# Second mixer: an order of their own for VectorE and ScalarE

## What is computed

```python
def sliding_window_sink_attention(q, k, v, sinks):      # 2 blocks of 128 queries, 16 heads on 4 kv heads
    ...
        sc = jnp.einsum('bqhgd,bkhd->bhgqk', qi, ki) * scale
        sc = jnp.where(valid, sc, -jnp.inf)
        mx = jnp.maximum(jnp.max(sc, axis=-1), sink)
        p = jnp.exp(sc - mx[..., None])
        denom = jnp.sum(p, axis=-1) + jnp.exp(sink - mx)
        return jnp.einsum('bhgqk,bkhd->bqhgd', (p / denom[..., None]), vi)

def swa_memory_mixer(...):
    q, q_mem = jnp.split(rms_norm(h, norm_w) @ in_w, [Q_WIDTH], axis=-1)
    q = partial_rope(q.reshape(bsz, s, Q_HEADS, HEAD_DIM), positions)       # rotates 16 of each head's 64
    att = sliding_window_sink_attention(q, k_sh, v_sh, sinks)
    m = memory_cross_attention(q_mem, mem, mem_norm_w, mem_w_kv)            # 4 heads over 256 memory tokens
    return jnp.concatenate([att, m], axis=-1) @ out_w
```

## Time and profile before

| | before |
|---|---|
| median of 3 runs | 1348.51 us (1348.46 to 1349.13) |
| the profiled execution | 1347.25 us |
| its span | 1345.4 us |
| mean granted TensorE clock | 0.964 |
| TensorE busy | 1217.9 us, 91% of the span |
| VectorE, ScalarE, GpSimd busy | 278.3, 210.3, 32.6 us |
| DMA | 463.03 MB, mean 344 GB/s |

### The profile page before, as it was taken

The page is one execution under the profiler, slowest core; times in us unless marked ns, Lnnn a source line. Parts: engine busy times, 40 slices in busy tenths (PEclk is TensorE's granted clock), DMA queues, the critical chain, the costliest instruction groups (busy, mean ns, idle before and its releaser), DMA issues. The chain is left out here.

```text
span 1345.4 us, 15098 instructions
## 1 busy us (share of the span) xinstructions
PE 1217.9 (91%) x6036; PEld 606.6 (45%) x6036; DVE 278.3 (21%) x679; ACT 210.3 (16%) x498; POOL 32.6 (2%) x42
## 2 busy tenths in 40 slices
PE   6999999999999999967777999999999999966785
PEld 5874775544444443532323475554444444322221
DVE  3841552131111111010101235241111111100101
ACT  2223332110000000000003235330010000000002
POOL 0001210000000000000000011100000000000000
PEclk9999999999999999989797999999999999978797
DMA  9830169579999999999999371389999999999994
GB/s 360 329 125 25 48 239 423 189 307 426 427 426 425 428 427 423 426 424 427 427 426 355 146 294 51 118 355 423 421 425 427 426 427 425 426 427 427 426 426 186
DMA packets 81241, 463.03 MB, mean 344 GB/s; under 512 B 7392, under 2 KB 9488, under 8 KB 32016
## 3 DMA queue, kind: packets, MB, share of 16 engines
q1 hardware_dynamic: 81168, 462.02, 83.1%
HBM read 460.91 MB, written 1.07 MB: 343 GB/s over the span
## 5 line engine op out<-in xcount | busy, mean ns | idle before, releaser
L1515 PE MATMUL bank<-own,work 128*64 128x512 f32 (+1 forms) x1176 | 281.0, 616 | 27.3 <-DMA own<-in_w_up 10.5
L1515 PEld LDWEIGHTS bank<-own,work 128*64 128x64 f32 (+1 forms) x1176 | 80.9, 128 | 166.6 <-issue 166.6
L1515 PE MATMUL bank<-late,work 128*32 128x512 f32 (+1 forms) x536 | 141.4, 626 | 12.3 <-DMA own<-in_w_up 12.3
L1524 PE MATMUL bank<-own,work 128*32 128x512 f32 (+1 forms) x416 | 113.5, 671 | 24.1 <-DMA h<-in_w_down 10.6
L1403 DVE TENSOR_TENSOR work<-work,bank 128x512 f32<-128x512 f32 x24 | 25.5, 1063 | 489.2 <-ACT work L1454 489.2
L1490 PEld LDWEIGHTS bank<-work,xs 128*128 128x128 f32 x768 | 89.4, 192 | 19.0 <-issue 19.0
L1490 PE MATMUL bank<-work,xs 128*128 128x128 f32 x768 | 95.5, 278 | 0.0
L1454 ACT ACTIVATE work<-bank 128x512 f32<-128x512 f32 x24 | 14.3, 597 | 518.8 <-PE bank L1515 518.8
L1507 PE MATMUL bank<-work 128*128 128x512 f32 x192 | 86.5, 593 | 1.4 <-ACT work L1464 1.4
L1524 PE MATMUL bank<-late,work 128*64 128x512 f32 (+1 forms) x256 | 76.6, 718 | 11.4 <-DMA late<-in_w_down 5.1
L417 PE MATMUL bank<-xnT,own 128*128 128x256 f32 x384 | 84.8, 380 | 0.0
(11 more groups left out here) (321 smaller groups left out, 1380.4 us busy)
## 6 DMA issues: line engine op xcount, KB each, us to landing
own<-in_w_up SPq DMA_DIRECT2D x81, 1024.0 KB, 13.0
own<-in_w_gate SPq DMA_DIRECT2D x66, 1024.0 KB, 12.3
own<-in_w_down SPq DMA_DIRECT2D x52, 1024.0 KB, 15.2
late<-in_w_gate SPq DMA_DIRECT2D x36, 1024.0 KB, 13.3
late<-in_w_down SPq DMA_DIRECT2D x32, 1024.0 KB, 13.8
late<-in_w_up SPq DMA_DIRECT2D x31, 1024.0 KB, 15.3
own<-in_a_in_w SPq DMA_DIRECT2D x17, 1024.0 KB, 13.4
h<-in_w_down SPq DMA_DIRECT2D x12, 1024.0 KB, 13.8
```

Source lines behind the costliest of these rows:

```text
L1515: ins = pe.matmul(bank[q * T:(q + 1) * T, :], self.xg[:, at:at + T], cut(tile(q), k=4)[:, k, :], start=(half == 0 and k == 0), stop=(half ...
L1524: ins = pe.matmul(self.b_down[out][q * T:(q + 1) * T, :], self.turned[:, at:at + T], cut(tile(q), j=2)[:, j, 512 * out:512 * out + 512], s ...
```

## The change

Two lists are added beside `order`: ScalarE walks `act_order` and VectorE `dve_order`. TensorE and the bank allocation keep `order`, which is as before. In the new lists some keys of `between[n]` stand one step later, behind the as of step n + 1: for ScalarE sc, for VectorE sc, q and kv. On VectorE, as n now begins with `inverse(n - 1)` in place of `inverse(n - 2)`, and only the inverse of the last part stands at its aT. `memory_softmax(h)` itself stays where it was, at the as of the step that has pT h.

```diff
--- before.py
+++ after.py
@@ -1661,15 +1661,21 @@
                    [("sc", 0)], [("rows0", 0), ("sc", 1)], [("pT", 0), ("rows0", 1)], [("pv", 0), ("sc", 2)], [("pT", 1), ("rows0", 2)],
                    [("pv", 1), ("sc", 3), ("rows0", 3)], [("pT", 2)], [("pv", 2), ("pT", 3)], [("rows0", 4)],
                    [("pv", 3), ("rows1", 4)], [("out", 0), ("out", 1), ("rows1", 5)], [("rows1", 0), ("rows1", 1)]]
+        act_order, dve_order = list(order), list(order)
+        act_later, dve_later = [], []
         for n in range(NA + 3):
-            if n < NA:
-                order += [("as", n)]
-            order += between[n]
-            if 2 <= n < NA + 2:
-                order += [("aT", n - 2)]
-            if n >= 3:
-                order += [("av", n - 3)]
+            scores = [("as", n)] if n < NA else []
+            parts_due = [("aT", n - 2)] if 2 <= n < NA + 2 else []
+            parts_due += [("av", n - 3)] if n >= 3 else []
+            order += scores + between[n] + parts_due
+            act_now, dve_now = ([key for key in between[n] if key[0] not in late] for late in (("sc",), ("sc", "q", "kv")))
+            act_order += scores + act_later + act_now + parts_due
+            dve_order += scores + dve_later + dve_now + parts_due
+            act_later, dve_later = ([key for key in between[n] if key[0] in late] for late in (("sc",), ("sc", "q", "kv")))
+        tail = len(order)
         order += [("x2T", 0), ("x2T", 1), ("rows1", 2), ("router", 0), ("out", 2), ("out", 3), ("x2T", 2), ("x2T", 3), ("router", 1), ("places", 0)]
+        act_order += order[tail:]
+        dve_order += order[tail:]
         holds = {key: [("out", 2 * t + half) for half in range(2)] for key in order for t in range(NT) if key[0] == f"rows{t}"}
 
         def freed(kind, i):
@@ -1736,7 +1742,7 @@
         def _(act):
             for q in (2, 3):
                 act.activation(*copy_h(c, 0, q), ACT.Copy).then_inc(s["h_act"], 1)
-            for key in order:
+            for key in act_order:
                 kind, i = key
                 if kind in ("out",) + Router.KINDS:
                     R.act(act, key)
@@ -1934,7 +1940,7 @@
 
             for q in (0, 1):
                 dve.tensor_copy(*copy_h(c, 0, q)).then_inc(s["h_dve"], 1)
-            for key in order:
+            for key in dve_order:
                 kind, i = key
                 if kind in ("out",) + Router.KINDS:
                     R.dve(dve, key)
@@ -1964,8 +1970,8 @@
                     dve.wait_ge(s["q_ev"], i + 1)
                     turn(chain(s["qr_dve"], 4 * i), cut(qtok[:, 512 * i:512 * i + 512], h=8), i // 2, 8)
                 elif kind == "as":
-                    if i >= 2:
-                        inverse(i - 2)
+                    if i >= 1:
+                        inverse(i - 1)
                     for kind2, h in between[i]:
                         if kind2 == "pT":
                             memory_softmax(h)
@@ -1984,7 +1990,7 @@
                     step(dve.tensor_tensor(col[:, k:k + 2], col[:, k:k + 2], sinks, ALU.max))
                     step(dve.tensor_scalar(col[:, k + 2:k + 4], col[:, k:k + 2], -1.0, None, ALU.mult))
                     step(dve.tensor_tensor(col[:, k + 6:k + 8], sinks, col[:, k:k + 2], ALU.subtract))
-                elif kind == "aT" and i >= NA - 2:
+                elif kind == "aT" and i == NA - 1:
                     inverse(i)
                 elif kind == "sc":
                     U.wait_done(dve, key)
```

## The result

| | before | changed |
|---|---|---|
| median of 20 runs each | 1349.11 us | 1355.13 us |
| ratio of the runs | | 1.0037, 95% interval 1.0027 to 1.0046 |
| the profiled execution, its span | 1347.25, 1345.4 us | 1355.44, 1353.6 us |
| attention stage in the trace | 128.08 us | 135.46 us |

What follows compares the result with a forecast made beforehand. The prediction took the second mixer's attention to be bound by TensorE; waits of +2.35 us plus +2.0 us for the clock made +4.35 us, so 1348.51 became 1352.9 us, with a range of 1350.4 to 1355.2 us.

Steps and rivals of the forecast that it cites:

- Part 1: Rotations a step later on VectorE: the transposes of qT and kT still get them in time, gain and cost 0.
- Part 2: Inverse with the next part's scores on VectorE: it waits for ScalarE's third exponential, delaying pT 1's softmax, +0.27 us.
- Part 3: Memory softmax's maximum and exponentials later: pT 0 -0.92, av 6 +0.37, av 10 +3.61 (sc banks freed later), pv 2 -0.98 us.
- Part 4: TensorE's granted clock falls to 0.50 after the stall before av 10, +2.0 us, bounds 0 and 3.0.
- the last rival: More stalls: av 8 later, a longer clock fall or a second one from av 6 and pT 1; +7 us, 1355.5 us, chance 0.09.
- One to one to the end: The mixer's shift passes whole to the end, since the second MoE's full DMA stretch waits for buffers TensorE frees after it.
- the stall without a fall: TensorE stalls before av 10 but the granted clock stays up: +2.35 us, 1350.9 us, chance 0.09.
- no bank wait: av 10's bank is free in time, only pT 2's late eviction is left: +0.7 us, 1349.2 us, chance 0.08.
- all waits gone: TensorE's waits before pT 0, pT 1 and pv 2 go with no new one: -3.14 us, 1345.4 us, chance 0.04.

Runs made afterwards that it cites:

- e1: Kernel before with only the rotations (q, kv) a step later on VectorE; ratio to the kernel before 0.9993 (0.9979 to 1.0006).
- e3: Kernel before with only the memory softmax's maximum and exponentials (sc) a step later on VectorE and ScalarE; ratio to the kernel before 1.0019 (1.0009 to 1.0029).
- e2: Kernel before with only a part's inverse moved to the next part's scores; ratio to the kernel before 1.0024 (1.0012 to 1.0036).
- e5: Changed kernel with two PSUM banks traded, av 10 taking av 9's and pv 2 sc 3's; ratio to the kernel before 1.0007 (0.9995 to 1.0019).
- f4: Changed kernel with four unread filling matmuls on TensorE ahead of av 10; ratio to the kernel before 1.0000 (0.9986 to 1.0014).
- f5: Changed kernel with unread filling matmuls on TensorE, four ahead of av 10 and two ahead of pT 1; ratio to the kernel before 1.0013 (1.0000 to 1.0025).
- f1: Changed kernel with seven unread filling matmuls on TensorE ahead of av 10; ratio to the kernel before 1.0032 (1.0017 to 1.0047).
- g1: Kernel before with memory softmax ahead of the inverse on VectorE and pT evictions ahead of the step's exponentials on ScalarE; ratio to it 0.9965 (0.9952 to 0.9978).
- e4: Changed kernel with sc 3 back in its old place on VectorE and ScalarE; ratio to the kernel before 1.0005 (0.9993 to 1.0017).
- f2: Changed kernel with unread filling matmuls on TensorE, seven ahead of av 10 and three ahead of pT 1; ratio to the kernel before 1.0051 (1.0038 to 1.0064).
- g2: Kernel of g1 with kv 1 computed ahead of as 0; ratio to the kernel before 0.9962 (0.9950 to 0.9974), median 1345.5 us.

## Why the prediction was right

- **Part 1, rotations at nothing:** shown (e1).
- **Part 2, +0.27 us at pT 1:** 0.36 us in the trace (1.60 against 1.24). The step is right for the change as a whole, but the price left out what the inverse costs elsewhere. Against e3, which moves sc and keeps the old inverse, the wait is 1.29 us longer (1.60 against 0.31): moving sc would have won 0.93 us at pT 1, which the sum didn't have, and the new place of the inverse takes that too. Alone it makes the wait before pT 0 longer and one before pT 3 new (e2); the pT 3 one I hadn't seen at all. In the changed kernel other parts of the change hide both.
- **Part 3, the banks:** -0.92, +0.37, +3.61 and -0.98 us were forecast; the trace has -0.92, +0.36, +3.57 and -0.98. av 5 and av 8 don't wait, as taken. That it is the bank is shown by e5. Sum of the waits: +2.35 forecast, +2.40 found, +2.45 in the stage of f4.
- **Part 4, the clock, +2.0 us:** right in kind, too small for the profiled execution. Behind the stall 3.4 us were lost in the profiled execution, above the 3.0 that I had as the bound. A second fall, behind the 1.60 us before pT 1, cost 1.7 us; I had this only in the last rival ("a second one from the waits at av 6 and pT 1"). The profiled execution is that rival: +7.38 us in the stage. Over the runs the clock's part is 5.0 - 2.4 = 2.6 us, an inference from the ratio that f5 supports. That 4.35 comes so near 5.0 us is therefore luck in part: the case that the sum describes, one fall of 2.0 us, is not what the trace shows.
- **The rows behind part 4** were read short. The trace of before has twelve idle times of 3.75 us or more behind its start, not eight; the four left out end between 575.63 and 659.34. It also has six of 2.04 to 2.99 us (187.61, 585.43, 629.91, 649.56, 731.59, 1196.46), and the clock fell within 1.1 us behind five of them, not behind the one at 187.61. Summed as above, four of these five falls make 1.7 us each, as do five of those at the longer idle times; the others make 3.4 us, one 5.1. So the trace of before already had idle times well under 3.75 us with a fall behind them. The one at 585.43 and its clock:

```profile
585.43 4.91 PE L1524 MATMUL bank<-own,work 128*32 128x512 f32 x28 [2.08 <-DMA own<-in_w_down]
```

```profile
585.00:590.00 5.00, 4.57 (x28) 1.59 (x32) 0.00 (x0) 0.00 (x0) 0.00 (x0) 0.66 1.02 431
```

- **One to one to the end:** shown. The DMA's idle stretch moved by some 8 us, as the stage's end did (888.13 to 896.86), and behind the stage the span has the same length (457.3 and 456.7 us). It is 456.9 to 457.5 us in e3, e5 and f1 too, with stages of 132.4 to 132.9 us. In the other experiments it is 458.1 to 460.7 us, beside a fall of the clock behind the stage that is told below.

The rivals: the stall without a fall, no bank wait, and all waits gone are each excluded by the trace of the changed kernel.

## What to carry to other kernels

Where units share a rotation of PSUM banks, an eviction that is put off is put off for the unit that takes the bank next; list who that is before moving it, and look for one with nothing long between. An idle time in a stream that TensorE bounds can cost twice, once itself and again in the clock behind it (3.57 us and 3.4 us here); the shorter ones did so in some traces only. What frees an operand for TensorE (a softmax ahead of its transposes, an eviction ahead of its product) should stand ahead of work with slack on the same engine, which is what g1 does.

## What the runs showed of the hardware

Idle times of TensorE shorter than I had thought were followed by a fall of the clock, and the same one wasn't always. Behind 1.59 to 1.60 us before pT 1 the clock fell in three traces (changed, e2, e5) and stayed at 1.00 in three (e4, f1, f4). Behind 2.08 us (e5) and behind 3.57 us (changed, e3) it fell each time, behind 1.24 us (before, e1) it didn't. A fall cost 1.7 us in the stage behind the shorter ones and 3.4 us behind 3.57 us. Outside the stage it is the same: before the first matmul of the second MoE, TensorE idles 1.28 to 1.29 us in every trace, behind several shorter idle times, and there the clock fell in nine traces (e1, e2, e4, f2 to f5, g1, g2) and stayed at 1.00 in five. e1, then before:

```profile
896.91 2.58 PE L1533 MATMUL bank<-small 128*128 128x512 f32 x3 [1.28 <-PEq L1642]
```

```profile
896.00:902.00 6.00, 5.09 (x19) 3.15 (x20) 3.69 (x20) 1.28 (x1) 0.00 (x0) 0.72 1.00 423
```

```profile
896.00:902.00 6.00, 5.02 (x33) 4.09 (x34) 4.46 (x21) 1.28 (x1) 0.00 (x0) 1.00 1.02 429
```

From the end of the stage to the end of the span, the five without this fall take 456.7 to 457.5 us and the nine with it 458.1 to 460.7. So falls that come and go are one part of what separates single executions of one kernel; how large a part isn't shown. The Trainium skill (TensorE: Matmul & The Clock Gate, "HAM oscillation") names waits of some microseconds as what lets the clock fall; these traces agree for 3.57 us and show that less than half of that can be enough.

The memory softmax on VectorE, whose two inputs lie in SBUF, takes longer beside GpSimd's scaling. The rows of both in the changed kernel, around pT 1:

```profile
826.37 0.16 DVE L1932 TENSOR_TENSOR work<-work 128x2 f32<-128x2 f32 x1 [1.32 <-ACT work L1775]
...
826.96 1.43 DVE L1939 TENSOR_TENSOR late<-late,work 128x512 f32<-128x512 f32 x1
```

```profile
826.81 1.04 POOL L1738 TENSOR_TENSOR late<-late,work 128x512 f32<-128x512 f32 x1 [5.27 <-DVE work L1933]
```

GpSimd ends at 827.85, and the softmax at 828.39, 0.54 us later; alone it takes 0.69 us (g1). The Trainium skill (SBUF — State Buffer, "Who interferes with whom") says that a VectorE instruction with two SBUF inputs contends with a GpSimd instruction that reads SBUF, for a port pair that is an exclusive lock. The rows agree: VectorE began 0.15 us behind GpSimd, and the 0.54 us behind GpSimd's end are most of the 0.69 us that it takes alone.
